# A run-in of attention between the last qkv units, with the sample's work four slots ahead of the prompt's instead of five

## What is computed

```python
for l in range(2):
    mix = rec_mixer if l == 0 else attention      # retention || RG-LRU, then dilated attention
    out_p, out_s = mix(rmsnorm(yp)), mix(rmsnorm(ys))
    yp = swiglu_block(yp + out_p); ys = swiglu_block(ys + out_s)
# attention: q, k, v = split(h @ w_in); q, k = head_rms(q), head_rms(k)      16 heads of 64
# prompt: three dilated bands over the 1024 tokens
# sample: each of 8 x 8 queries gathers keys from its own cache of 2048 positions and the new rows
```

## Time and profile before

| | |
|---|---|
| median of 3 runs | 2923.31 us (2922.74 to 2925.38) |
| the profiled execution | 2926.86 us, its span 2925.1 us |
| TensorE, matmuls | busy 2860.0 us, 98% of the span |
| VectorE / ScalarE / POOL | busy 1357.5 / 784.4 / 117.3 us |
| mean granted clock of TensorE | 0.997 |
| last qkv unit ends, first prompt scores | 1534.87, 1558.49 us |

### The profile page before, as it was taken

One profiled execution on the slowest core, in us unless ns is written; L12 is line 12 of the kernel. 1 busy time (PEld: TensorE's weight loads), 2 busy tenths in 40 slices (PEclk: granted clock), 3 DMA queues, 4 the chain that ended last, 5 costly groups with the idle time before them and its releaser, 6 DMA issues.

```text
span 2925.1 us, 47558 instructions
## 1 busy us (share of the span) xinstructions
PE 2860.0 (98%) x21369; PEld 2721.0 (93%) x21369; DVE 1357.5 (46%) x1756; ACT 784.4 (27%) x1240; POOL 117.3 (4%) x218
## 2 busy tenths in 40 slices
PE   7999999999999999999998999998999999999999
PEld 7999999999999999999996766767999999999999
DVE  5754543444444444745403555556444444444444
ACT  5444522111111111322215444444221111111111
POOL 1010000000000000000001111110000000000000
PEclk9999999999999999999999999999999999999999
DMA  5120211111111111222338667763111111111111
GB/s 191 44 67 18 105 58 44 44 44 44 44 44 44 44 44 44 105 75 90 105 119 277 206 204 251 249 191 124 53 44 44 44 44 44 44 44 44 44 44 62
DMA packets 126249, 253.80 MB, mean 87 GB/s; under 512 B 7585, under 2 KB 88693, under 8 KB 125536
## 3 DMA queue, kind: packets, MB, share of 16 engines
q1 hardware_dynamic: 112960, 189.29, 19.7%
q0 software_dynamic: 11776, 56.96, 5.7%
q10 hardware_dynamic: 1312, 4.52, 0.5%
HBM read 222.72 MB, written 28.02 MB: 86 GB/s over the span
## 4 chain that ended last, share of the span: by engine, by line
PE 92%; DVE 2%; ACT 2%; DMA 2%; SPq 1%; issue 0%; POOL 0%; ACTq 0%; POOLq 0%; DVEq 0%
PE psum L223 64%; PE psum L482 14%; PE psum L1899 3%; PE psum L1956 2%; PE psum L1914 2%; PE psum L1878 2%; PE psum L1927 1%; DMA cache_tile<-in_cache_k 1%; ACT smp_kt L2010 1%; SPq L1849 1%; PE psum L1980 1%; PE psum L591 1%; DMA x_natural<-in_x_prompt 0%; PE psum L1903 0%; DVE att_pt L2081 0%; ACT att_scores L2027 0%
## 5 line engine op out<-in xcount | busy, mean ns | idle before, releaser
L223 PE MATMUL psum<-h_hi,w_hi 128*128 128x364 f32 (+1 forms) x2568 | 568.4, 330 | 0.9 <-DVE h_lo L1199 0.9
L223 PE MATMUL psum<-h_lo,w_hi 128*128 128x364 f32 (+1 forms) x2568 | 565.4, 328 | 0.0
L223 PE MATMUL psum<-h_hi,w_lo 128*128 128x364 f32 (+1 forms) x2568 | 562.9, 327 | 0.0
L223 PEld LDWEIGHTS psum<-h_hi,w_hi 128*128 128x128 f32 x2568 | 443.8, 188 | 4.3 <-issue 1.1
L223 PEld LDWEIGHTS psum<-h_hi,w_lo 128*128 128x128 f32 x2568 | 444.2, 188 | 0.0
L223 PEld LDWEIGHTS psum<-h_lo,w_hi 128*128 128x128 f32 x2568 | 444.1, 188 | 0.0
L205 ACT ACTIVATE w_hi<-w_raw 128x2048 fp32r<-128x2048 f32 x96 | 183.5, 1912 | 660.7 <-PE psum L223 609.2
L482 PE MATMUL psum<-w_hi,h_hi 128*128 128x256 f32 (+1 forms) x1152 | 325.8, 283 | 0.0
L482 PE MATMUL psum<-w_hi,h_lo 128*128 128x256 f32 (+1 forms) x1152 | 323.6, 281 | 0.0
L482 PE MATMUL psum<-w_lo,h_hi 128*128 128x256 f32 (+1 forms) x1152 | 322.9, 280 | 0.0
L1518 DVE TENSOR_TENSOR x_res<-x_res,psum 128x1092 f32<-128x1092 f32 x176 | 227.3, 1292 | 200.3 <-PE psum L223 200.3
(11 more groups left out here) (318 smaller groups left out, 3225.4 us busy)
## 6 DMA issues: line engine op xcount, KB each, us to landing
cache_tile<-in_cache_k SPq DMA_DIRECT2D x64, 512.0 KB, 8.2
cache_tile<-in_cache_v SPq DMA_DIRECT2D x64, 512.0 KB, 6.2
w_raw<-in_w_ffn_gate SPq DMA_DIRECT2D x22, 1024.0 KB, 4.9
w_raw<-in_w_ffn_up SPq DMA_DIRECT2D x22, 1024.0 KB, 5.0
w_raw<-in_w_ffn_down SPq DMA_DIRECT2D x22, 1024.0 KB, 4.8
w_raw<-in_w_in_att SPq DMA_DIRECT2D x12, 1024.0 KB, 7.1
w_raw<-in_w_in_rec SPq DMA_DIRECT2D x10, 1024.0 KB, 4.9
park_x<-x_res POOLq DMA_DIRECT2D x2, 4368.0 KB, 14.0
```

The costliest lines, as they stand in the source:

```text
L223: mm = pe.matmul(PS[:, bank + c, 0:n], st[:, slot, wc:wc + P], mv[:, k, c * CW:c * CW + n], start=(i < NCH), stop=(i >= 3 * NCH * nk - NCH))
```

## The change

The sample's work leads the prompt's by four slots (`LEAD = 4`). The whole lead-in, slots -4 to -1 with four places each, is issued between the last 16 qkv units, one place behind each of the units 92 to 107, on TensorE and on ScalarE. To free banks 4 and 5 for the turns, these units use five banks only (`LATE`). POOL's loads move with it: the samples' rows and the first pair before the store of block 8, the first v, a small bias for the first three slots (`att_bias_first`) and the second pair's q and k before the store of block 11; the first sample's new v row moves from SyncE's queue to POOL's. Buffers move accordingly. At the start, VectorE splits block 0 one tile earlier, the last squares come behind columns 2 and 3 instead of 0 and 1, the root before column 6 instead of 4, `x_mean` and `prep_inverse` before columns 4 and 6 instead of 2 and 4, and the spread behind the last column and inside the second tile.

```diff
@@ s1_dve, first_tile, hook, rec_act, rec_dve
-            if n == 3:
+            if n == 2:
                 split_lo(dve, 0, 0)
...
+                if f == 1 and k == 1:
+                    prep_spread(pe, q2, SPREAD[2:])
...
-                    if k == 5:
+                    if k == KT - 1:
                         prep_spread(pe, q2, SPREAD[:2])
-                    if k == KT - 1:
-                        prep_spread(pe, q2, SPREAD[2:])
...
+            if k == KT - 2:
                 prep_root(act, 0, fm=False)
-                act.wait_ge(xt_a, N_BOTH)
             prep_hi(act, q2, G_MIX[0], k)
-            if k < N_BOTH:
-                x_square(act, NT - N_BOTH + k)
+            if k in (2, 3):
+                x_square(act, NT - N_BOTH + k - 2)
...
-            if k == 2:
+            if k == 4:
                 x_mean(dve)
-            if k == 4:
+            if k == 6:
                 prep_inverse(dve, 0)
@@ the qkv stage
+    LATE = (0, 1, 2, 3, 6)
+    U_RUN = NT * N_QKV - 16
+    u_bank = [BANKS[u % NB8] if u < U_RUN else LATE[(u - U_RUN) % len(LATE)] for u in range(NT * N_QKV)]
+    def run_in(u):
+        return -LEAD + (u - U_RUN) // 4, (u - U_RUN) % 4 + 1
...
+                    if u >= U_RUN:
+                        step(*run_in(u))
...
+                    n, f = run_in(u)
+                    for i in phase(n, f):
+                        take_act(act, n, i)
...
-            if j == 9:
+            if j == 8:
                 for i in range(2):
                     pool.wait_ge(v_dma[i], 32 * 4)
                 pool.dma_start(QSN[:, :], qtok[SEQ:SEQ + NS, :]).then_inc(b_ld, 16)
...
+            if j == N_QKV - 2:
+                pool.wait_ge(t_out[0], 1)
+                pool.wait_ge(t_out[1], 1)
+                q_blocks(0)
+            if j == N_QKV - 1:
+                pool.wait_ge(v_dma[0], 32 * (N_QKV // 2))
+                load_v(0)
+                pool.dma_start(BIF[:, :, :], a["c_bp"][0:2]...).then_inc(a_bf, 16)
+                bank, count = qk_last(0)
+                pool.wait_ge(t_out[bank], count)
+                load_qk(1)
@@ attention
-    LEAD = 5
+    LEAD = 4
+    N_RUN = 0
...
+    def phase(n, f):
+        nt = len(turns(n))
+        return range(2 * f - 2, min(2 * f, nt) if f < 4 else nt)
...
+        def step(n, f):
+            b, s = sample_slot(n)
+            if 0 <= n < NSLOT and f == 1:
+                scores(n)
+            for i in phase(n, f):
+                turn(n, i)
+            if 2 <= n and f == 1:
+                pv(n - 2)
+            for t in SCORED.get((s, f), ()):
+                tile_scores(b, t)
+            sample_pv(b, WEIGHED.get((s, f), ()))
...
-        for n in SLOTS:
+        for n in SLOTS[N_RUN + LEAD:]:
```

More of the change, by code:

```diff
@@ L1582, in build, with bank_left @@
     NB8 = len(BANKS)
+    LATE = (0, 1, 2, 3, 6)
+    U_RUN = NT * N_QKV - 16
+    u_bank = [BANKS[u % NB8] if u < U_RUN else LATE[(u - U_RUN) % len(LATE)] for u in range(NT * N_QKV)]
+    u_last = [max([x for x in range(u) if u_bank[x] == u_bank[u]], default=None) for u in range(NT * N_QKV)]
+    def bank_left(bank):
+        return max(u for u in range(NT * N_QKV) if u_bank[u] == bank) + 1
+    def run_in(u):
+        return -LEAD + (u - U_RUN) // 4, (u - U_RUN) % 4 + 1
     NB8P = 3
@@ L1588, in first @@
             prep_wait(pe, q8, "hl_in", k + 1)
+        step = att_pe(pe)
         for j in range(N_QKV):
@@ L1748, in build @@
     KNB = at("smp_k_new", w + 26688, [P, HP, DS])
-    VN = [at(f"att_v{i}", w + o, [P, QT, P]) for i, o in enumerate((13824, 5632))]
+    VN = [at(f"att_v{i}", w + o, [P, QT, P]) for i, o in enumerate((0, 13824))]
     ADG = at("att_diag", w + 41504, [P, 2, 2, P])
@@ L1850, in cache_load @@
                                  src[name][P - 32:P, b, t + 2 * x, :]).then_inc(b_tile[j % 8], 16)
[L1851 to L1856, removed]
+            if u == 8 and b:
+                sp.wait_ge(b_vu, 10 * b)
                 sp.dma_start(VNB[:, :], a["v_sample"][0][b:b + 1].rearrange("a s h d -> (a s) (h d)")).then_inc(b_vn, 16)
@@ L1871, in scores @@
                 pe.wait_ge(a_red, 2 * n)
+            else:
+                pe.wait_ge(v_out, NT * N_QKV)
             if qb == 0:
@@ L1983, in sample_pv, with s9_pe @@
                     mm.then_inc(b_vu, 1)
-        pe.wait_ge(v_out, NT * N_QKV)
+        def step(n, f):
[9 more added lines that the diff above has]
+            sample_pv(b, WEIGHED.get((s, f), ()))
+        return step
+    def s9_pe(pe):
+        step = att_pe(pe)
@@ L1986, in s9_pe @@
         for n in SLOTS:
[L1987 to L1990, removed]
             for f in range(1, 5):
[L1992 to L1998, removed]
@@ L2000, in s9_act @@
-    def s9_act(act):
[L2001 to L2021, removed]
@@ new lines, in s9_pe, with take_act @@
+                if n >= N_RUN:
+                    step(n, f)
+    def take_act(act, n, i):
+        what, x, c = turns(n)[i]
+        g = T0[n] + i
+        bank = PS[:, 4 + g % 2, :]
+        act.wait_ge(t_in[g % 2], g // 2 + 1)
+        if what in ("qs", "ks"):
+            act.activation((QTS, KTN)[what == "ks"][:, :, :].rearrange("p a w -> p (a w)"), bank,
+                           ACT.Copy).then_inc(t_out[g % 2], 1)
+        elif what == "k":
+            act.activation(SKT[:, x % 2, 4 * c:4 * c + 4, :].rearrange("p a w -> p (a w)"), bank,
+                           ACT.Copy).then_inc(t_out[g % 2], 1)
+        elif what == "qk":
+            t = (QH, KH)[c // 2][x % 2]
+            act.activation(t[:, (c % 2) * 512:(c % 2 + 1) * 512], bank, ACT.Copy).then_inc(q_hi, 1)
+        else:
+            for e in range(2):
+                r = slice(e * DH, (e + 1) * DH)
+                dst = OX[r, :, S0 + 4 * x * DS:S0 + (4 * x + 4) * DS].rearrange("p k (b q) -> p b k q", q=DS)
+                src = bank[r, :].rearrange("p (b k e q) -> p b k e q", b=4, e=2, q=DS)[:, :, :, e, :]
+                op = act.activation(dst, src, ACT.Copy)
+            op.then_inc(t_out[g % 2], 1)
@@ L2034, in s9_act @@
             for i in mine[0:2]:
-                take(n, i)
+                take_act(act, n, i)
             if s == 6:
@@ L2082, in take @@
                 elif c < 2:
+                    if x == 0 and c == 0:
+                        for y in range(2):
+                            dve.wait_ge(v_dma[y], 32 * (N_QKV // 2))
                     op = dve.tensor_copy(PTS[:, 4 * c:4 * c + 4, :].rearrange("p a w -> p (a w)"), bank)
@@ L2110, in s9_dve @@
                 dve.wait_ge(a_s, n + 1)
-                if n % QT == 0:
+                if n == 0:
+                    dve.wait_ge(a_bf, 16)
+                if n == NBF or n and n % QT == 0:
                     dve.wait_ge(a_bl[n // QT % 2], 16 * (n // QT // 2 + 1))
@@ L2171, in q_blocks @@
                 pool.wait_ge(b_sc, 5 * b)
-            done = 2 + 5 * b
+            done = 2 + 5 * b if b else 1
             for hpar in range(2):
```

66 lines of the change are left out of this document (37 added, 29 removed).

## The result

| | before | after |
|---|---|---|
| median of 5 runs | 2925.38 us (2922.74 to 2927.23) | 2938.78 us (2937.59 to 2941.57) |
| the profiled execution, its span | 2926.86 us, 2925.1 us | 2937.73 us, 2936.0 us |

The ratio is 1.0043 [1.0032, 1.0054]: slower by 0.43%, 13.4 us between the medians and 10.9 us between the profiled spans. The forecast was +8.5 us, 2931.8 in a range of 2914 to 2947.

The account below looks back on a forecast made before the run. TensorE, busy 98% of the span, bounds the kernel; only its waits and low-clock stretches can move time. Head -7.7, rotation +16.6, start +1.1, tail -1.5 sum to +8.5: 2931.8 us against the median 2923.31, eight in ten 2914 to 2947.

Parts of the forecast that it names:

- rotation: Six attention rounds: the sample's steps lie one slot later beside other work, waits add 2.76 us a round, +16.6 us.
- head: Last qkv unit to slot 4: sample's work moved between units shortens the 54.2 us, -7.7 us, between -10 and -1.
- start: Kernel start: first tile done 1.35 us earlier, but the first gate's evacuation later, +1.1 us, between -1.5 and +2.5.
- tail: End of attention: last sample ends one slot nearer the prompt's end, less wait for its last tile, -1.5 us, -3.5 to +1.
- The waits laid out for slots 0 to 3: Head, slots 0 to 3 with the sample's steps 4 to 7: work and waits together put at 26.5 us.
- Second slot: Round's second slot, now step 5: second q turn waits 0.31 us, p turn 1.24, sum 1.55.
- third slot: Round's third slot, now step 6: TensorE waits 0.42 us for the low part and 0.54 for the exponentials, 0.96.
- the 0.2 laid out for cache tiles: Rounds: last v tile and next sample's first key tile meet a slot 0.27 us shorter, +0.2 a round.
- a rival that comes in every round: Clock falls in every round, slots two and three idling 3.5 us: +8 to +30, 2940 to 2962 us; chance 0.12.
- the prediction's own last sentence: Forecast wrong if rounds stay within 0.5 us of 58.2, run-in waits exceed 0.5, or the clock falls where it now doesn't.
- The gain in the first tile: Start: VectorE splits block 0 a tile earlier, first tile done 1.35 us earlier, 0.33 us of spread still owed: -1.0.
- small ScalarE steps hang on the last spread: Start: three small LRU steps and two table loads come 1.4 us later, delaying the first gate's evacuation: +2.1 us.

Follow-up runs that it names:

- run 1: The kernel before with LEAD = 4 and nothing else, no run-in and the old start: 2943.36 us, 1.0059 to the kernel before.
- run 3: The kernel after with the next pair's q and k turns one slot later, in slots 3 and 4 of a round: 2925.1 us, 0.9996 to the kernel before.
- run 10: The kernel before with LEAD = 4 and the q and k turns one slot later, no run-in, old start: 2928.92 us, 1.0007 to the kernel before.
- run 9: The kernel after with the q and k turns one slot later and the start's edits taken back: 2924.65 us, 0.9985 to the kernel before.
- run 8: The kernel before with LEAD = 3 and nothing else: 2944.68 us, 1.0058 to the kernel before.
- run 7: The kernel after with the last part of the spread back inside the first tile, beside the other two: 2938.66 us, 1.0036 to the kernel before.
- run 4: The kernel after, but in second slots ScalarE takes all three turns before the second exponential: 2938.4 us, 1.0036 to the kernel before.
- run 6: The kernel after with the start of the kernel before: 2939.44 us, 1.0035 to the kernel before.
- run 5: The kernel before with the edits at the start alone: 2927.84 us, 1.0004 to the kernel before.
- run 11: The kernel after with LEAD = 5, slots -5 to -2 in the run-in's 16 units, and the old start: 2924.3 us, 0.9991 to the kernel before.
- run 2: The kernel after with LEAD = 5, all five lead-in slots behind the last 20 units: 2929.03 us, 1.0009 to the kernel before.

## Why the prediction was right, point by point

**Direction and cause: right.** Slower, by the rotation, less a gain in the head. Run 1 shows that the rotation alone does it, run 3 that the place of the q and k turns carries most of it: with them moved along, six rounds take 353.8 us, 5.1 over before instead of 18.8. The size was forecast short: +8.5 us against 13.4 between the medians, and the sum came as near as it did in the profiled execution partly by luck (start and tail, below). Its terms, in us:

| term | predicted | profiled execution |
|---|---|---|
| head | -7.7 | -7.45 |
| six rounds | +16.6 | +18.8, of which 15.3 at full clock and 3.5 by the clock |
| start | +1.1 | +2.1 |
| the rest, by subtraction | -1.5 | -2.6 |
| sum | +8.5 | +10.9 |

**Head.** The waits in the run-in are 1.7 us in three, against 1.75 laid out; units weren't held up, the clock stayed at 1.00. (The waits laid out for slots 0 to 3 and their work add to 26.35, not 26.5; it moves the head by 0.15.) Run 10 against 9 bears a gain of the run-in out in timed runs; that the whole -7.45 is the run-in it isn't (4.75 against run 1).

**Rotation: right in place, a little over-sized.** Second slot 0.31 + 1.24 laid out, 0.25 + 1.04 measured; third slot 0.42 + 0.54 and 0.39 + 0.54. A round at full clock is 60.54 to 60.77 us: 2.55 over the 58.12 of before, where 2.76 was laid out; six make 15.3. Two small things were off and nearly cancel: 0.35 for `smp_pt` in the third slot was not laid out, and the 0.2 laid out for cache tiles did not come (5.5 us in all, 5.8 before).

**The clock: the step that failed.** It was given nothing in the sum, and a chance of 0.12 as a rival that comes in every round. By the prediction's own last sentence the forecast fails here, for the clock fell where it did not before. It came in three of six (slots 16, 32 and 40 onward): the granted clock fell to 1.2 GHz within the third slot, which then takes 10.71 us instead of 9.08. Ahead of the fall the engine had waited 0.25, 1.04, 0.39, 0.54, 0.35 and 0.70 us in two slots, and the same six waits stand in the three rounds without a fall. The three rounds with a fall are 61.83 us on average against 60.67: 1.16 each, 3.5 in all. The price was read about rightly from the earlier trace rows (1.4 us a fall); wrong was to argue that waits of this kind, spread over the slots, leave the clock alone.

The other runs bear this out. The new order's third slot (or the fourth, in run 8) has such a fall in three rounds of six after and in runs 1 and 8, in one in runs 3, 7 and 9, in two in run 10, and in none in runs 4 and 6. The other falls in the rounds, one each in runs 4, 5, 6 and 8 and two in run 11, came beside a single wait of 1.9 to 2.5 us for a cache tile, in the old order (5 and 11) as in the new. The Trainium skill ("TensorE: Matmul & The Clock Gate", section "HAM oscillation — how this bites in real kernels") tells of a loop that waits some 3 to 5 us for a DMA behind every tile and whose clock falls in every one. No round here has a wait of that length; at the short ones of this kernel the fall came in some rounds only.

**Start: inside its bounds, its two halves not resolved.** The gate's wait of 2.1 came in the place named. The gain in the first tile that was to pay for half of it can't be read from single executions: the first qkv matmul stood anywhere from 1225.48 to 1229.35 over all runs, with the edits (1226.15 in run 5, 1228.79 after) as without. By the ratios of runs 5, 6 and 9 the start costs 1 to 3 us, none of it clear of noise; that the profiled +2.1 stands near the forecast +1.1 says nothing. The step "small ScalarE steps hang on the last spread" was right for 0.4 of the 2.1 us only (run 7).

**Tail: right in this execution, by luck.** The last tile's wait shrank from 2.11 to 0.35, and no clock fell there:

```profile
2004.12 0.64 PE L2026 MATMUL psum<-cache_tile,smp_pt 128*32 128x256 f32 x8 [0.35 <-DMA cache_tile<-in_cache_v]
```

But the same wait in run 4, where the tail is the same, is

```profile
2004.10 0.64 PE L2026 MATMUL psum<-cache_tile,smp_pt 128*32 128x256 f32 x8 [2.00 <-DMA cache_tile<-in_cache_v]
```

with a fall of the clock behind it. In run 1 it is 1.81, in run 6 0.86, in run 7 1.25. From slot 56 to the out-projection it is 56.43 us after, and 57.33 to 60.01 in those four runs; with the old order it is 57.38 before and 56.13 to 56.54 in runs 2, 5 and 11. The new order has one step of the sample more in that stretch, 2.1 us by the prediction's unit costs (an estimate). With that taken off, the two orders overlap, so the shorter tail that the prediction reasoned out is not shown.

**What stays open.** The medians differ by 13.4 us, the profiled executions by 10.9; the 2.5 between can't be placed in one profile each, though the short tail of that execution points the same way. What varies between profiled executions is seen: waits for cache tiles in the rounds are 5.5 us after, 10.0 in run 4 and 9.1 in run 6, whose rounds have nearly the same work, and the low clock comes at other places and in other numbers. Why, no run here tells, nor why the same waits bring a fall in one round and not in the next.

## What to carry to other kernels

Shifting one stream against another by a slot moves no work and still costs, where engines serve both in a fixed order: before such a shift, lay out for each slot that changes kind which copy frees which bank, what stands ahead of it on its engine, and which long row of matmuls had been hiding it. Let what shares those queues shift along (here two turns, one slot: 13.7 us in the time, 5.0 of it by the waits that were worked out). And separate the terms by runs early: the part that looked like the change (the run-in, some 5 to 6 us of gain) was hidden under a number that came with it.

## What the runs showed of the hardware that was not expected

- Short waits can cost clock without a long one: after, 3.27 us of waits in two slots, none over 1.04, came ahead of each fall to half the clock in three rounds of six, and in the other three of none. In runs 3, 9 and 10 four falls in 18 rounds came behind waits of 0.47, 0.39, 0.54, 0.35 and 0.70. The 24 rounds of the old order (before, runs 2, 5 and 11) have three falls, each beside one wait of 1.9 to 2.5 us.
- A fall costs less than its slot shows: the slot grew by 1.63 us, the round by 1.16, since the slot behind it waits less for its v tile.
- A block stored by POOL and loaded back took 8.4 us from the store's issue to the load's; for 6.98 of them POOL did nothing else (run 2).
